# The hybrid stage of a three-block transformer kernel: 14 diagonal taps instead of 31, and its first weight piece halved ahead

## The reference, cut to what matters

```python
z = h @ w_in + b_in                      # conv_a, conv_gate, q, k, v, o: 512 columns each, and 8 gate columns
u = conv_a * sigmoid(conv_gate)
u = causal_depthwise_conv(u, conv_w, conv_b)      # 31 taps, 512 channels
u = silu(layernorm(u, conv_ln_g, conv_ln_b))
qk = silu(causal_depthwise_conv(concat(q, k), qk_conv_w, qk_conv_b))   # 4 taps
ht = mlstm_chunkwise(q, k, v, i_pre, f_pre)       # 4 heads of 128
hm = headwise_norm(sigmoid(o) * ht) * mlstm_norm_g
return concat(u, hm) @ w_out
```

## Time and profile before

| | us |
|---|---|
| median of 3 runs | 2307.43 (2303.1 to 2310.71) |
| the profiled execution, its own time | 2304.43 |
| its span | 2302.8 |
| PE busy | 2126.4 (92%) |
| DVE busy | 1362.7 (59%) |
| ACT busy | 1085.3 (47%) |
| odd phase ends, hybrid stage begins | about 1400 |
| output product (L714) begins | 1627.57 |

### The profile page before, as it was taken

How to read it: one execution, slowest core, us unless ns; L and a number is a source line. 1 busy time by engine, 2 the same in 40 slices (tenths; PEclk the granted TensorE clock), 3 DMA queues, 4 the chain that set the end, 5 groups by cost and what they waited for, 6 DMA issues and landing times. The chain is left out here.

```text
span 2302.8 us, 27998 instructions
## 1 busy us (share of the span) xinstructions
PE 2126.4 (92%) x10084; PEld 1713.4 (74%) x10084; DVE 1362.7 (59%) x1759; ACT 1085.3 (47%) x1200; POOL 172.9 (8%) x237
## 2 busy tenths in 40 slices
PE   7999899999998999699999997899878999999993
PEld 5777578888886777488888885686457788888882
DVE  3442246555436555556464446766346889988994
ACT  3326524343322445424343324364225788788883
POOL 2001110000001000100000000000012111111111
PEclk9999999999998999699999998899979999999997
DMA  8232028732323221223332322320128999999994
GB/s 223 69 87 75 19 74 299 213 92 92 110 81 94 65 65 65 74 83 92 98 104 92 110 73 66 91 74 1 41 89 317 382 413 411 411 415 409 411 397 182
DMA packets 223574, 377.38 MB, mean 164 GB/s; under 512 B 12604, under 2 KB 174716, under 8 KB 201080
## 3 DMA queue, kind: packets, MB, share of 16 engines
q1 hardware_dynamic: 206280, 315.21, 39.6%
q0 software_dynamic: 17200, 60.89, 7.1%
HBM read 339.84 MB, written 38.84 MB: 164 GB/s over the span
## 5 line engine op out<-in xcount | busy, mean ns | idle before, releaser
L1004 PE MATMUL PS<-XS,split 128*128 128x512 f32 (+1 forms) x2304 | 482.3, 372 | 3.6 <-DVE XS L154 3.1
L1004 PEld LDWEIGHTS PS<-XS,split 128*128 128x128 f32 x2304 | 406.6, 188 | 79.1 <-DVE XS L154 3.6
L154 DVE TENSOR_TENSOR moe_split<-moe_raw,moe_split 128x2048 fp32r<-128x2048 f32 x174 | 397.3, 2289 | 64.3 <-ACT moe_split L149 62.6
L154 DVE TENSOR_TENSOR split<-ring,split 128x2048 fp32r<-128x2048 f32 x111 | 254.1, 2292 | 281.8 <-ACT split L149 281.7
L2562 PE MATMUL PS<-moe_split,moe_x 128*128 128x512 f32 x1392 | 341.3, 398 | 4.8 <-DVE moe_split L154 4.8
L149 ACT CAST moe_split<-moe_raw 128x2048 fp32r<-128x2048 f32 x174 | 332.7, 1913 | 24.3 <-DMA moe_raw<-in_expert_w_gate 14.6
L149 ACT CAST split<-ring 128x2048 fp32r<-128x2048 f32 x112 | 213.1, 1904 | 204.8 <-PE PS L1040 116.6
L2562 PEld LDWEIGHTS PS<-moe_split,moe_x 128*128 128x128 f32 x1392 | 260.3, 190 | 57.9 <-DVE moe_split L154 5.2
L2584 PE MATMUL PS<-moe_split,moe_h 128*128 128x512 f32 x696 | 164.9, 393 | 2.0 <-DVE moe_h L154 2.0
L2584 PEld LDWEIGHTS PS<-moe_split,moe_h 128*128 128x128 f32 x696 | 130.5, 189 | 31.7 <-DVE moe_h L154 2.2
L1040 PE MATMUL PS<-split,XS 128*128 128x512 f32 x672 | 152.6, 389 | 0.0
(11 more groups left out here) (355 smaller groups left out, 2558.9 us busy)
## 6 DMA issues: line engine op xcount, KB each, us to landing
moe_raw<-in_expert_w_gate SPq DMA_DIRECT2D x58, 1024.0 KB, 7.4
moe_raw<-in_expert_w_up SPq DMA_DIRECT2D x58, 1024.0 KB, 8.3
moe_raw<-in_expert_w_down SPq DMA_DIRECT2D x58, 1024.0 KB, 7.3
ring<-in_w_up SPq DMA_DIRECT2D x88, 512.0 KB, 5.1
ring<-in_w_down SPq DMA_DIRECT2D x44, 512.0 KB, 4.4
expert_rows<-rows POOLq DMA_DIRECT2D x4, 4096.0 KB, 30.8
expert_rows<-W POOLq DMA_DIRECT2D x29, 512.0 KB, 8.4
ring<-in_w_in SPq DMA_DIRECT2D x24, 512.0 KB, 5.3
```

What stands on the lines that cost most here:

```text
L154: return dve.tensor_tensor(lo, raw, hi.bitcast(F32), ALU.subtract)
L1004: mm = pe.matmul(PS[:, b + q, rows], w[:, c, q, :], x_half(k, high)[:, c, rows], start=(c == 0 and m == 0), stop=(c == KC - 1 and m == 2))
```

## The change

`DIAGONAL = 14`: of group 3's taps PE takes 14 instead of 31, DVE 16 and ACT's seed one. `make_diagonals` and `convolve_last` run once; nothing of them is left after head 3. DVE adds PE's bank to its accumulator (`add_last`). The taps are spread anew over DVE's queue. The first piece is halved in the phase before. ACT takes `silu_qk(0)` ahead of the sigmoid of `og`.

```diff
 def hybrid_ahead(k):
+    first_high = k.sem("hybrid_first_high")
+    product, slot = k.tail.product, k.cv_slabs[0][0]
...
+    def early_scalar(act):
+        act.wait_ge(product, NT)
+        slab_ready(k, act, k.cv_slabs[0])
+        split_high(k, act, k.ring[:, slot, :], k.split[:, 0, 1, :], first_high)
+
+    def gpsimd(pool):
+        pool.wait_ge(first_high, 1)
+        split_low(pool, k.ring[:, slot, :], k.split[:, 0, 1, :], k.split[:, 0, 0, :]).then_inc(k.freed[slot], 1)
+
+    k.tail.early = early = Namespace()
+    early.scalar, early.vector = early_scalar, lambda dve: None
+    return dict(sync=sync, gpsimd=gpsimd)
...
+    DIAGONAL = 14
+    diagonal = [W[:, i * P:(i + 1) * P] for i in range(DIAGONAL)]
...
+        def convolve_last():
+
+            pe.wait_ge(s.diagonals, 1)
+            pe.wait_ge(s.kept, 2 * HL)
+            for i in range(DIAGONAL):
+                mm = pe.matmul(PS[:, 7, :], diagonal[i], u[:, 3, i:i + S], start=(i == 0), stop=(i == DIAGONAL - 1))
+            mm.then_inc(s.last_conv, 1)
...
-                convolve_last(0, 16)
+                convolve_last()
...
-        convolve_last(16, CW)
         pe.wait_ge(s.acc_done, 4)
...
-        high_w(act, 0)
+        act.sem_inc(s.w_high, 1)
...
-            if c < 3:
-                begin_acc(c)
+            begin_acc(c)
...
+        silu_qk(0)
         act.wait_ge(s.vo_raw, 2)
         act.activation(og[:, 0, :, :], og[:, 0, :, :], ACT.Sigmoid).then_inc(s.og_done, 1)
-        silu_qk(0)
...
-                make_diagonals(0, 16)
-            if h == 3:
-                act.wait_ge(s.projected, 3 * HL)
-                make_diagonals(16, CW)
+                make_diagonals()
...
-        act.wait_ge(s.last_conv, 1)
-        act.activation(acc[:, 3, :], PS[:, 7, :], ACT.Identity, bias=wide_b[:, 3:4]).then_inc(s.acc_done, 1)
...
-        taps = iter([(c, i) for c in range(3) for i in range(PAD)])
+        taps = iter([(c, i) for c in range(4) for i in range(DIAGONAL if c == 3 else 0, PAD)])
...
+        def add_last():
+
+            dve.wait_ge(s.last_conv, 1)
+            dve.drain()
+            dve.tensor_tensor(acc[:, 3, :], PS[:, 7, :], acc[:, 3, :], ALU.add).then_inc(s.acc_done, 1)
...
-        low_w(dve, 0)
...
         make_u(1)
-        convolve(7)
+        convolve(3)
         low_w(dve, 5)
-        convolve(4)
+        convolve(6)
         make_u(2)
         convolve(6)
...
         low_w(dve, 7)
-        convolve(6)
+        convolve(9)
         convolve_qk(0, 0)
+        convolve(2)
+        convolve_qk(0, 1)
         low_w(dve, 8)
-        convolve_qk(0, 1)
-        convolve(8)
+        convolve(4)
         keep_vo(0)
         for h in range(HL):
-            convolve(4)
+            convolve((9, 7, 7, 6)[h])
...
             if h + 1 < HL:
+                convolve(2)
                 convolve_qk(h + 1, 0)
-                convolve(4)
+                convolve(3)
                 convolve_qk(h + 1, 1)
+            else:
+                convolve(4 * PAD)
+                add_last()
             if h < 2:
                 low_w(dve, 10 + 2 * h)
             else:
-                convolve(4)
+                convolve(5)
...
             mm.then_inc(s.varied, 1)
+            convolve(2)
             dve.wait_ge(s.rooted, h + 1)
...
-        convolve(4 * PAD)
         for t in range(NT):
             norm_c(t)
```

More of the change, by code:

```diff
@@ L1248, in sync @@
             load_slab(k, sp, k.cv_slabs[c], [columns(k.A["w_in_2"][0], c * P + 512 * q, P) for q in range(2)])
-    return dict(sync=sync)
+    def early_scalar(act):
[8 more added lines that the diff above has]
+    return dict(sync=sync, gpsimd=gpsimd)
 def diff_stage(k):
@@ L1639, in hybrid_stage @@
     ln_g, ln_b, head_g = k.chan[:, 184:188], k.chan[:, 188:192], k.chan[:, 192:196]
-    diagonal = [W[:, i * P:(i + 1) * P] if i < 16 else k.XT[:, (i - 16) // 4, (i - 16) % 4 * P:(i - 16) % 4 * P + P]
-                for i in range(CW)]
+    DIAGONAL = 14
+    diagonal = [W[:, i * P:(i + 1) * P] for i in range(DIAGONAL)]
     place = [(0, 0), (1, 0), (2, 0), (1, 384)]
@@ L1648, in hybrid_stage @@
              "exped cut weighted valued v_read varied rooted normed y_turned y_out acc_done c_turned "
-             "c_varied c_rooted c_normed c_back c_out w_high split_used gw_split qk_begun acc_begun diagonals "
-             "last_conv scaled").split()
+             "c_varied c_rooted c_normed c_back c_out w_high split_used gw_split qk_begun acc_begun scaled "
+             "diagonals last_conv").split()
     s = Namespace()
@@ L1655, in hybrid_stage @@
      s.varied, s.rooted, s.normed, s.y_turned, s.y_out, s.acc_done, s.c_turned, s.c_varied, s.c_rooted,
-     s.c_normed, s.c_back, s.c_out, s.w_high, s.split_used, s.gw_split, s.qk_begun, s.acc_begun, s.diagonals, s.last_conv,
-     s.scaled) = (k.sem("hy_" + n) for n in names)
+     s.c_normed, s.c_back, s.c_out, s.w_high, s.split_used, s.gw_split, s.qk_begun, s.acc_begun, s.scaled, s.diagonals,
+     s.last_conv) = (k.sem("hy_" + n) for n in names)
     k.hy_y_out, k.hy_c_out = s.y_out, s.c_out
@@ L1893, in leave_y, with make_diagonals @@
             act.mul(YT[:, 4 + h, :], PS[:, 1, :], head_g[:, h:h + 1]).then_inc(s.y_out, 1)
-        def make_diagonals(first, end):
-            for i in range(first, end):
+        def make_diagonals():
+            for i in range(DIAGONAL):
                 mm = act.mul(diagonal[i], k.ident, wide[:, i, 3:4])
@@ L2004, in convolve_qk @@
             mm.then_inc(s.convd, 1)
-        taps = iter([(c, i) for c in range(3) for i in range(PAD)])
+        taps = iter([(c, i) for c in range(4) for i in range(DIAGONAL if c == 3 else 0, PAD)])
         def convolve(n):
             for c, i in itertools.islice(taps, n):
-                if i == 0:
+                if i == (DIAGONAL if c == 3 else 0):
                     dve.wait_ge(s.acc_begun, c + 1)
@@ L2016, in convolve @@
                                               acc[:, c, :], ALU.mult, ALU.add)
-                if i == PAD - 1:
+                if i == PAD - 1 and c < 3:
                     mm.then_inc(s.acc_done, 1)
+        def add_last():
+            dve.wait_ge(s.last_conv, 1)
+            dve.drain()
+            dve.tensor_tensor(acc[:, 3, :], PS[:, 7, :], acc[:, 3, :], ALU.add).then_inc(s.acc_done, 1)
         def keep_vo(h):
```

## The result

The changed kernel took 2286.73 us (median of 5 runs, 2286.07 to 2291.66) against 2307.43; the ratio is 0.992 (95% interval 0.9904 to 0.9937), which is a gain of 18.5 us (14.5 to 22); forecast were 16.5 and 2290.9 us. Twelve later runs gave 2291.17 against 2303.26 and a ratio of 0.9948 (0.9933 to 0.9963), a gain of 12 us (8.5 to 15.4). So the time alone says 12 to 18 us, and single runs scatter by more than the parts of this sum (2282.70 to 2298.66 in those twelve). The profiled execution took 2286.19 us, with a span of 2284.6.

What follows compares the result with a forecast made beforehand. PE, 92% busy, bounds the kernel; savings elsewhere count only where it waits. A gain of 18.9 us at the first norm, less 1.35 and 1.0, leaves 16.5: 2290.9 us, range 2287 to 2297, wider 2283 to 2299.

Steps and rivals of the forecast that it cites:

- Step 1: Hybrid stage entry: first piece halved ahead, POOL holding DVE's L876 3.3 us; PE starts 1.0 us earlier (0.7 to 4.3).
- Rival B: Tail and heads: POOL doesn't hold DVE and the clock stays; gain 22.3 us, 2285; chance 0.10.
- Step 2: Fourth `u`: fewer DVE taps ahead, wait 2.1 us, `project_qk(0)` 11.16 us at full clock; gain there 5.0 us.
- Step 3: First head: SiLU ahead of the sigmoid, broadcast 8.9 us earlier, half the 3.2 us of half clock regained; gain 10.4.
- rival A: Reopened PE waits: the clock falls in each; gain only 7 to 10 us, about 2299; chance 0.11.
- Step 4: Heads 0 to 3: `leave_y` late behind DVE's taps, losing 1.2 us in head 1 and 1.8 in head 2.
- Step 5: Last block on PE: fewer diagonals save 1.7 us in head 3, then 9.8 before the token norms.
- Step 6: Way out to the output product: late first root costs 1.35 us, possible half clock there 1.0.
- The end moves by the same: Behind the output product: no instruction changes, so the kernel's end moves by the same 16.5 us.
- Rival C: Heads: DVE's 64 serial taps become the bound; at 1.3 us per tap, 2319 us, slower than before; chance 0.03.
- Rival D: Heads: taps near 1.0 us and part of the clock loss; 3 to 5 us left, 2303; chance 0.06.

Runs made afterwards that it cites:

- three edits: Low half of first piece on DVE, head 0's SiLU before the gate-column copy, `leave_y` before the scaled output, against the changed kernel: 2278.49 us, then 2281.58.

## Why the prediction was right

*Step 1* had the mechanism: gain 0.65, forecast 1.0. POOL's subtraction blocked L876 just as in the odd block, and taking POOL away (high half early, low half late) gave the 3.3 us back. The Trainium skill's rule on the port pair (SBUF — State Buffer, "Who interferes with whom") agrees here, 4.58 against 1.28 us. It also shows in the heads: POOL's four selects took 1.50 and 1.53 us beside taps in heads 1 and 2, and 1.02 in head 3, where DVE stood waiting for them. In head 1 DVE's weights still started right behind its last tap (1526.06), so the price was 0, as taken. Rival B (no hold) is out.

*Step 2* had the position (wait 1.83, forecast 2.1) but not the clock: `project_qk(0)` took 12.76, not 11.16, so the gain behind it was 3.2 and not 5.0. No run isolates the two taps fewer ahead of the fourth `u`. *Step 3* too: half clock after 2.83 us of idle cost all of the 3.2 us, where half was taken back. Together 3.5 of the forecast 10.4 failed to come, 3.1 of it by the clock. This is rival A at two places; the third (output product at half clock, -1.0) did not happen: the clock had fallen at 1603 but was back at 1.00 by 1610, and the block took 14.00. The whole of rival A (7 to 10 us left at the output product) is out.

*Step 4* named the right waits with the right cause and priced them too high: 0.3 and 1.3 against 1.2 and 1.8. In head 1 the reason can be read off. The worked-out count had `scaled` 28.1 us after broadcast 1; it came 27.3 after it, since DVE's steps were a little shorter and began 0.2 ahead of the broadcast. In the run with the early SiLU `scaled` came 28.2 after the broadcast and the head took 30.5 us, where 30.6 had been worked out. But that agreement is partly luck: DVE there waited 0.99 us for the selects, because ACT was late with the exponentials, a wait that the count did not hold. That PE came late out of head 0 at half clock, and so left ACT and DVE more room, fits both runs. Head 2 was the same 30.4 us in both, apart from the 1.7 that the clock cost with the early SiLU; forecast were 31.0, so there the count itself was 0.6 too long. *Step 5* came out as summed (11.6 from broadcast 3 to the first norm, forecast 11.5), and putting the diagonals back undid 11.0 at that point. *Step 6*: -1.2 against -1.35 for the late root; moving `leave_y` and the root won back 0.55 and 0.63 of it.

So the sum at the output product (15.8, forecast 16.5) is close partly because errors cancel: the gain up to broadcast 1 was put 3.5 us too high, nearly all of it the clock, and the losses in the heads and on the way out were put 2.5 us too high as well. "The end moves by the same" was wrong: the second block of the output product lost 1.7 to the clock (15.70 after the same 2.56 us wait that cost nothing before), so that 14.0 us reached the router. The stretch behind the router then came out 3.9 us shorter, which the second profile of the same kernel did not repeat (604.3 us, as before). That the end of the profiled span moved by 18.0 us, and so looks like more than was forecast, is luck; the later twelve runs, with 12 us (8.5 to 15.4), stand on the other side of 16.5.

Rival C had the right mechanism only at 8 diagonals, where DVE does set the end of head 3. In the kernel as changed the taps stayed 0.82 us apart. Rival D (3 to 5 us left) lies below both intervals of the time.

## What to carry to other kernels

Moving work from the bounding engine to a lighter one pays where its last piece stood alone on the path: here 15 diagonals behind head 3 and 2 inside it were worth 11.0 us at the first norm and 9.7 at the output product. Before work is hung on POOL in a stage's tail, look at which two-input DVE instruction will meet it, and ask whether the consumer needs all of it at once: the high half alone was enough to start PE. A small step queued behind a long one on a helper engine (`leave_y` behind the scaled output) decides what a gain further up is worth; move it first, or the gain is given back. And count a gain at the last common position that repeats, here the router: a gain at the output product could still be lost to the clock on the 71 us between them, as it was with the early root.

## What the runs showed of the hardware that was not expected

- Short PE waits can cost the clock. In the twelve profiles of edited or changed kernels the wait of 1.8 to 2.2 us ahead of `project_qk(0)` cost it every time. The wait of 1.53 to 1.55 us ahead of broadcast 3 cost it in one profile (scores 4.63 us) and not in six (2.42 us). The wait of 2.56 us ahead of the output product's second block cost it in six (15.70 us instead of 14.00) and not in the other six, nor before. What decides was not tested. Two profiles of one kernel agreed at each of these places, in both pairs. So such waits are priced from both sides, 0 to 3.4 us each here.
- The same kernel's time from router to end differed by 8.4 us between two executions (three edits), more than most edits here were worth, while the 225 us ahead of the output product repeated within 0.4 us (0.7 at most between kernels that are the same up to the point compared).
